# Modulation, first norm and first projections of a hybrid diffusion layer, moved into one block of engine programs

## The reference, cut to what matters

```python
mod = jax.nn.silu(c) @ w_mod[i] + b_mod[i]                 # 1024 -> 6144
mod_c = jax.nn.silu(c_ctx) @ w_mod[i] + b_mod[i]
sh1, sc1, gt1, sh2, sc2, gt2 = jnp.split(mod[:, None, :], 6, axis=-1)
h = rmsnorm(x, norm1_w[i]) * (1 + sc1) + sh1
hc = rmsnorm(ctx, norm1_w[i]) * (1 + csc1) + csh1
y, yc = mixer(h, hc, ...)            # begins with h @ w_in, conv, silu, l2norm, rotary of q, k, v
x = x + gt1 * y
h2 = rmsnorm(x, norm2_w[i]) * (1 + sc2) + sh2
x = x + gt2 * expert_choice_ffn(h2, ...)
# in the mixer, the Fourier branch:
y = jnp.fft.fftn(ug, axes=(1, 3), norm='ortho').real
```

## Time and profile before

| what | value |
|---|---|
| median of three runs | 4763.62 us |
| the profiled execution | 4760.79 us |
| its span (first to last instruction) | 4759.3 us |
| mean granted clock of TensorE over it | 0.936 |
| TensorE, VectorE, ScalarE, GpSimd busy | 86%, 46%, 31%, 9% |
| first projection (L356) starts at | 240.81 us |
| last block of the first tile is copied (L413) at | 273.87 us |

### The profile page before, as it was taken

How to read it: one execution, slowest core, us unless ns; L and a number is a source line. 1 busy time by engine, 2 the same in 40 slices (tenths; PEclk the granted TensorE clock), 3 DMA queues, 4 the chain that set the end, 5 groups by cost and what they waited for, 6 DMA issues and landing times. The chain is left out here.

```text
span 4759.3 us, 62227 instructions
## 1 busy us (share of the span) xinstructions
PE 4105.7 (86%) x22412; PEld 3244.3 (68%) x22412; DVE 2176.2 (46%) x2864; ACT 1498.3 (31%) x2447; POOL 451.1 (9%) x486
## 2 busy tenths in 40 slices
PE   6599997996896299999969999997915999999998
PEld 5244443444674188888857778786815999999997
DVE  0334441005563255555543553534486555555554
ACT  0323331012562022222222332322203444444443
POOL 0000000000011133333300000000000000000000
PEclk9799997998898699999979999998957999999999
DMA  5611112102102322222143434324405666676773
GB/s 209 223 38 58 57 44 78 35 9 67 22 8 56 84 67 78 68 79 79 58 154 120 148 98 158 95 78 166 150 18 191 213 210 214 209 218 201 219 213 102
DMA packets 237491, 546.60 MB, mean 115 GB/s; under 512 B 34154, under 2 KB 103434, under 8 KB 233610
## 3 DMA queue, kind: packets, MB, share of 16 engines
q1 hardware_dynamic: 210890, 446.08, 29.4%
q0 software_dynamic: 26432, 98.06, 6.9%
HBM read 444.25 MB, written 99.81 MB: 114 GB/s over the span
## 5 line engine op out<-in xcount | busy, mean ns | idle before, releaser
L2413 DVE TENSOR_TENSOR sb_we_low<-sb_we,sb_we_high 128x1024 fp32r<-128x1024 f32 x384 | 467.2, 1223 | 142.2 <-ACT sb_we_high L2365 142.0
L2365 ACT ACTIVATE sb_we_high<-sb_we 128x1024 fp32r<-128x1024 f32 x384 | 401.6, 1052 | 292.0 <-PE ey L2338 156.6
L356 PE MATMUL p_ps<-sb_hT,sb_wq 128*128 128x512 f32 (+1 forms) x960 | 380.3, 554 | 32.6 <-DMA sb_wq<-in_w_ch 32.6
L1737 PE MATMUL pg<-sb_hb_high,sb_wm_high 128*128 128x512 f32 x768 | 307.2, 400 | 40.9 <-DVE sb_hb_low L1854 40.9
L1849 DVE TENSOR_TENSOR sb_wm_low<-sb_wm,sb_wm_high 128x1024 fp32r<-128x1024 f32 x128 | 156.3, 1222 | 391.9 <-ACT sb_wm_high L1784 391.9
L356 PEld LDWEIGHTS p_ps<-sb_hT,sb_wq 128*128 128x128 f32 x960 | 184.9, 193 | 219.8 <-issue 180.3
L1738 PE MATMUL pg<-sb_hb_low,sb_wm_high 128*128 128x512 f32 x768 | 303.1, 395 | 0.0
L1739 PE MATMUL pg<-sb_hb_high,sb_wm_low 128*128 128x512 f32 x768 | 302.5, 394 | 0.0
L576 PE MATMUL z_ps<-sb_hT,sb_wz 128*128 128x512 f32 (+1 forms) x672 | 284.6, 587 | 14.8 <-DMA sb_wz<-in_w_ch 14.8
L2320 PE MATMUL eg<-sb_xe_high,sb_we_high 128*128 128x256 f32 x1024 | 289.0, 282 | 2.8 <-DVE sb_xe_low L2408 1.6
L2321 PE MATMUL eg<-sb_xe_low,sb_we_high 128*128 128x256 f32 x1024 | 286.7, 280 | 0.0
(11 more groups left out here) (351 smaller groups left out, 8705.6 us busy)
## 6 DMA issues: line engine op xcount, KB each, us to landing
sb_we<-in_w_ex SPq DMA_DIRECT2D x384, 512.0 KB, 4.4
sb_wm<-in_w_gates SPq DMA_DIRECT2D x96, 512.0 KB, 3.6
sb_wrow<-in_w_mod_row SPq DMA_DIRECT2D x16, 1024.0 KB, 5.1
sb_wm<-in_w_br SPq DMA_DIRECT2D x32, 512.0 KB, 4.5
sb_lq<-q_d SPq DMA_DIRECT2D x36, 256.0 KB, 2.7
sb_lk<-k_d SPq DMA_DIRECT2D x36, 256.0 KB, 2.9
sb_lkt<-kt_d SPq DMA_DIRECT2D x36, 256.0 KB, 3.6
sb_lvt<-vt_d SPq DMA_DIRECT2D x36, 256.0 KB, 4.3
```

The source lines that it names most:

```text
L356: last = nc.tensor.matmul(ps[:, b % BANKS, 0:wd], w[:, kind, k], g.hT[:, k, t0:t0 + wd], start=(k == 0), stop=(k == KD - 1))
L1737: nc.tensor.matmul(bank[:], high, rh[:, k], start=(k == ks[0]), stop=False)
L2365: nc.scalar.activation(wh[:, n % CUT], w[:, n % RAW], ACT.Copy).then_inc(s.wh, 1)
L2413: v.tensor_tensor(wl[:, n % CUT], w[:, n % RAW], wh[:, n % CUT], ALU.subtract).then_inc(s.wl, 1)
```

## The change

`load_tables`, `modulation` and `first_norm` are gone as stages; their work moves into the first window of `delta_inputs`, with no barrier between. In parts:

1. Columns: the two vectors silu(c), silu(c_ctx) become the stationary operand (two columns wide) and w_mod moves past it, 512 columns at a time: 8 x 4 matmuls (`mod_rows`) into four PSUM banks of two partitions. ScalarE and VectorE copy two each to SBUF, and sixteen small transposes turn them to columns (`mod_columns`). w_mod comes in eight DMAs of 1 MB over five slots that lie in tiles not yet used (`sl`, `turned`, `rsb`).
2. Loads: all on SP's queue, in one order: c, five w_mod parts, the first 512 columns of the constants, the small vectors, x of block 0, three more w_mod parts (each waits for a slot), x of block 1, weights of tile 0, x of blocks 2 to 4, weights of tiles 1 and 2, the rest of the constants; the rotary table after the last sum of the norm, since its tile holds the squares.
3. Norm: ScalarE squares a block in two halves, GpSimd adds each half to half its size, TensorE sums four parts instead of eight, ScalarE takes Ln and Exp (for root and reciprocal), VectorE multiplies in two halves; scaling and shifting is split, four parts on ScalarE, four on VectorE. TensorE projects the first tile block by block between the sums.
4. Rows: GpSimd multiplies 64 pieces of w_mod (128x512) by silu(c) per partition and adds them up, seven or eight pieces behind each of the nine weight loads, and stores eight partial rows (`rowp_d`).
5. Fourier loads the partial rows, the bias and norm2; TensorE sums over the partitions with the matrix of ones in eight matmuls, VectorE adds the bias; `rows_d` is stored there.

```diff
--- before.py
+++ after.py
...
-def delta_inputs(nc, g):
+def delta_inputs(nc, g, consts, eps):
...
+flat_sl, flat_tt = sl[:].rearrange("p a t -> p (a t)"), tt[:].rearrange("p n c -> p (n c)")
+wcol = [flat_sl[:, i * 2 * D:(i + 1) * 2 * D] for i in range(3)] + [flat_tt[:, 0:2 * D], rs[:, 0:2 * D]]
+SLOTS = len(wcol)
+sqr = rope[:].rearrange("p a t -> p (a t)").rearrange("p (u k t) -> p u k t", u=2, k=4)
+cols = cv[0:2, 0:2 * D]
 ps = psum(nc, c, "p_ps", (P, BANKS, 512))
...
+prow = [ps[0:2, 0], ps[0:2, 1], ps[0:2, 2], pr[0:2]]
...
+nrs = acc
...
+        def load_x(b):
+            t0, wd = BLOCKS[b]
+            sp.dma_start(g.hT[:, :, t0:t0 + wd], g.xT[:, :, t0:t0 + wd]).then_inc(s_x[b], 16)
+        sp.dma_start(cc[:], g.cc).then_inc(s.cld, 16)
+        for k in range(KD):
+            if k == SLOTS:
+                sp.dma_start(consts[:, 0:C_DIR], g.consts[:, 0:C_DIR]).then_inc(s.cst, 16)
+                sp.dma_start(bcol[:], g.b_mod_col).then_inc(s.small, 16)
+                sp.dma_start(n1[:], g.norm1).then_inc(s.small, 16)
+                load_x(0)
+            if k >= SLOTS:
+                sp.wait_ge(s.used, k - SLOTS + 1)
+            sp.dma_start(wcol[k % SLOTS], g.w_mod_col[:, k]).then_inc(s_wc[k % SLOTS], 16)
+        load_x(1)
+        sp.dma_start(w[:, 0], g.w_ch[0]).then_inc(s_wi[0], 16)
+        for b in range(2, NB):
+            load_x(b)
+        for kind in range(1, 3):
+            sp.dma_start(w[:, kind], g.w_ch[kind * H]).then_inc(s_wi[kind], 16)
         sp.dma_start(cw[:], g.conv_w).then_inc(s.tab, 16)
+        sp.dma_start(consts[:, C_DIR:C_W], g.consts[:, C_DIR:C_W]).then_inc(s.rest, 16)
+        sp.wait_ge(s.nsumh, 2 * NB)
         sp.dma_start(rope[:], g.rope).then_inc(s.tab, 16)
+        for b, (t0, wd) in enumerate(BLOCKS):
+            if b:
+                sp.wait_ge(s.ha, KH * (b + 1))
+                sp.wait_ge(s.hd, KH * (b + 1))
+                sp.dma_start(g.h_d[:, :, t0:t0 + wd], g.hT[:, :, t0:t0 + wd]).then_inc(s.hst, 16)
...
+        def add_squares(b):
+            wd = BLOCKS[b][1]
+            for j in range(2):
+                pool.wait_ge(s.nsq, 2 * b + j + 1)
+                nc.gpsimd.tensor_tensor(sqr[:, j, 0:2, 0:wd], sqr[:, j, 0:2, 0:wd], sqr[:, j, 2:4, 0:wd],
+                                        ALU.add).then_inc(s.nadd, 1)
+        def load_row(i):
+            k, at = i % KD, i // KD * 512
+            pool.dma_start(wrow[:, i % 2], g.w_mod_row[at // (2 * D) * KD + k][:, at % (2 * D):at % (2 * D) + 512]).then_inc(s_wr[i % 2], 16)
+        def row_part(i):
+            k, j = i % KD, i // KD
+            dst = acc[:, j % 2]
+            pool.wait_ge(s_wr[i % 2], 16 * (i // 2 + 1))
+            if k == 0:
+                if j < 2:
+                    pool.wait_ge(s.nmul, 2 * NB)
+                if j >= 2:
+                    pool.wait_ge(s_as[j % 2], 16 * (j // 2))
+                nc.gpsimd.tensor_scalar(dst, wrow[:, i % 2], cs[:, k, 0:1], None, ALU.mult).then_inc(s.part, 1)
+            else:
+                nc.gpsimd.tensor_scalar(wrow[:, i % 2], wrow[:, i % 2], cs[:, k, 0:1], None, ALU.mult).then_inc(s.scaled, 1)
+                pool.wait_ge(s.part, i)
+                pool.wait_ge(s.scaled, i - j)
+                nc.gpsimd.tensor_tensor(dst, wrow[:, i % 2], dst, ALU.add).then_inc(s.part, 1)
+            pool.wait_ge(s.part, i + 1)
+            if i + 2 < ROWP:
+                load_row(i + 2)
+            if k == KD - 1:
+                pool.dma_start(g.rowp_d[:, j * 512:(j + 1) * 512], dst).then_inc(s_as[j % 2], 16)
+        ROWP = 8 * KD
+        for b in range(NB):
+            add_squares(b)
+        tiles = [(h, kind) for h in range(H - 1) for kind in range(3)]
+        load_row(0)
+        load_row(1)
+        for n, (h, kind) in enumerate(tiles):
+            pool.wait_ge(s.proj, NB * (3 * h + kind + 1))
+            pool.dma_start(w[:, kind], g.w_ch[kind * H + h + 1]).then_inc(s_w[kind], 16)
+            for i in range(ROWP * n // len(tiles), ROWP * (n + 1) // len(tiles)):
+                row_part(i)
...
+            if isinstance(t, int) and t == 0:
+                pe.wait_ge(s.ha, KH * (b + 1))
+                pe.wait_ge(s.hd, KH * (b + 1))
...
+        def mod_rows():
+            pe.wait_ge(s.sc, 1)
+            for k in range(KD):
+                pe.wait_ge(s_wc[k % SLOTS], 16 * (k // SLOTS + 1))
+                for j in range(4):
+                    last = nc.tensor.matmul(prow[j], cs[:, k], wcol[k % SLOTS][:, j * 512:(j + 1) * 512],
+                                            start=(k == 0), stop=(k == KD - 1))
+                last.then_inc(s.used, 1)
+        def mod_columns():
+            pe.wait_ge(s.rowe, 4)
+            for m in range(2 * KD):
+                last = nc.tensor.transpose(pcol[:, m], cols[:, m * P:(m + 1) * P], g.ident[0:2, 0:2])
+            last.then_inc(s.colt, 1)
+        def norm_sums(b):
+            wd = BLOCKS[b][1]
+            wait(pe, s.nln, b - 1)
+            for j in range(2):
+                pe.wait_ge(s.nadd, 2 * b + j + 1)
+                for i in range(2):
+                    last = nc.tensor.matmul(pn[:, b % 2, 0:wd], g.ones, sqr[:, j, i, 0:wd],
+                                            start=(j == 0 and i == 0), stop=(j == 1 and i == 1))
+                last.then_inc(s.nsumh, 1)
         def window(new, one, two):
+            if new and not one:
+                mod_rows()
+                pe.wait_ge(s.cst, 16)
+                norm_sums(0)
+                mod_columns()
+                norm_sums(1)
+                norm_sums(2)
             for b in range(NB):
+                if new and not one and 0 < b < 3:
+                    norm_sums(b + 2)
                 if new:
                     project(*new, b)
                 if two and two[1] < 2 and b > 0:
...
+        act.wait_ge(s.cld, 16)
+        nc.scalar.activation(cs[:], cc[:], ACT.Silu).then_inc(s.sc, 1)
+        def squares(b):
+            t0, wd = BLOCKS[b]
+            act.wait_ge(s_x[b], 16)
+            for j in range(2):
+                wait(act, s.nsumh, 2 * (b - 1) + j + 1)
+                nc.scalar.activation(sqr[:, j, :, 0:wd], g.hT[:, j * KH:(j + 1) * KH, t0:t0 + wd], ACT.Square).then_inc(s.nsq, 1)
+        def inverse_root(b):
+            t0, wd = BLOCKS[b]
+            act.wait_ge(s.nsumh, 2 * b + 2)
+            wait(act, s.nmul, 2 * (b - 1))
+            nc.scalar.activation(nrs[:, b % 2, 0:wd], pn[:, b % 2, 0:wd], ACT.Ln, bias=g.eps[:, 0:1], scale=1.0 / D).then_inc(s.nln, 1)
+            act.wait_ge(s.nln, b + 1)
+            nc.scalar.activation(nrs[:, b % 2, 0:wd], nrs[:, b % 2, 0:wd], ACT.Exp, scale=-0.5).then_inc(s.nrs, 1)
+        def modulate(b):
+            t0, wd = BLOCKS[b]
+            which = 1 if b == 0 else 0
+            act.wait_ge(s.mod, 3)
+            act.wait_ge(s.nmul, 2 * b + 1)
+            for k in range(KH):
+                nc.scalar.activation(g.hT[:, k, t0:t0 + wd], g.hT[:, k, t0:t0 + wd], ACT.Identity,
+                                     bias=g.mod1[:, 0, k, which:which + 1],
+                                     scale=g.mod1[:, 1, k, which:which + 1]).then_inc(s.ha, 1)
...
         def window(new, one, two):
+            if new and not one:
+                squares(0)
+                for j in range(2):
+                    act.wait_ge(s.used, KD)
+                    nc.scalar.activation(cols[:, j * 512:(j + 1) * 512], prow[j], ACT.Copy).then_inc(s.rowe, 1)
+                act.wait_ge(s.eps, 1)
+                for b in range(1, NB + 2):
+                    if b < NB:
+                        squares(b)
+                    if b == NB + 1:
+                        act.wait_ge(s.zero, 1)
+                        copy_raw(*new, (0,))
+                    if b > 1:
+                        modulate(b - 2)
+                    if b <= NB:
+                        inverse_root(b - 1)
+                copy_raw(*new, range(1, NB))
+                return
             if new:
...
+        for j in range(2, 4):
+            dve.wait_ge(s.used, KD)
+            nc.vector.tensor_copy(cols[:, j * 512:(j + 1) * 512], prow[j]).then_inc(s.rowe, 1)
...
+        for b, (t0, wd) in enumerate(BLOCKS):
+            which = 1 if b == 0 else 0
+            dve.wait_ge(s.nrs, b + 1)
+            for j in range(2):
+                part = g.hT[:, j * KH:(j + 1) * KH, t0:t0 + wd]
+                nc.vector.tensor_tensor(part, part, nrs[:, b % 2, None, 0:wd].broadcast_to([P, KH, wd]), ALU.mult).then_inc(s.nmul, 1)
+            dve.wait_ge(s.nmul, 2 * b + 2)
+            for k in range(KH, KD):
+                nc.vector.tensor_scalar(g.hT[:, k, t0:t0 + wd], g.hT[:, k, t0:t0 + wd], g.mod1[:, 1, k, which:which + 1],
+                                        g.mod1[:, 0, k, which:which + 1], ALU.mult, ALU.add).then_inc(s.hd, 1)
         dve.wait_ge(s.tab, 32)
...
+        sp.dma_start(parts, g.rowp_d).then_inc(s.rp, 16)
```

(37 more changed lines are left out.)

190 lines of the change are left out of this document (23 added, 167 removed).

## The result

The changed kernel took **4623.31 us** (median of 4 runs, 4617.05 to 4625.03) against 4763.41 (4 runs), 0.9708 of the kernel before, interval [0.9696, 0.972]. The gain is 140 us, not 171; 4623 is just outside the range of 4581 to 4620. The profiled execution took 4625.03, its span is 4623.5. The front did what was forecast and a little more. Most of what is missing went 3.4 milliseconds later, in a stage that the change doesn't touch.

What follows compares the result with a forecast made beforehand. TensorE bounds the windows; a chain of engines working one at a time bounds the start. 4760.8 - 171.4 (block 4's earlier copy) + 3 (rotations) = 4592.4, said as 4592; range 4581 to 4620, own range 4583 to 4600 (62%).

Steps and rivals of the forecast that it cites:

- E: End of the column matmuls (`mod_rows`): 36.8 us, bounds 34 if fast from the start and 61.3 if slow throughout.
- the slow start: Column matmuls: TensorE runs at the slow clock for the first 5.8 us, adding 2.9 us to E.
- slow-columns rival: Columns: narrow stationary operand does not bring the clock up, E = 61.3, +24.5 us, 4617 in all; chance 15%.
- shared-landing rival: Columns: w_mod parts in flight share the engines and land together, 12 us later, 4605 in all; chance 7%.
- the walk: Norm and first projections, timed from E: ScalarE slowest at 10.6 us a block, block 4 copied at E + 65.7 = 102.5.
- slow start of 2.9 behind that wait: Projection of block 3: after 5.6 us idle awaiting block 0's copy, TensorE starts slow, +2.9 us.
- under 4: Sign to look for in the profile: GpSimd's row pieces take under 4 us each.
- The +3 for rotations: Windows: GpSimd's additions delay VectorE's last rotation before the transposes, once per head, +3 us within 0 to 11.
- contention rival: Windows: GpSimd and VectorE hold each other up at full price in rotations, +11 not +3, 4600 or 4611; chance 10%.
- at 0: Fourier stage: summing the partial rows takes 8 to 16 us in a gap of 86.67 us, so no cost.
- the rival said 25 to 40: Norm not run before columns, or first tile not before norm's end: 25 to 40 us of gain lost; chance 4%.
- My own mark: Wrong if the stretch from block 4's copy to the next stage's first projection is over 10 us longer.

Runs made afterwards that it cites:

- 155 early: Changed kernel with 155 more instructions in TensorE's program, in the Fourier stage's wait, restoring the code places of later loops: 4587.22 us.
- p_nopieces: Changed kernel with TensorE's code at the places of before and only the first of every eight GpSimd row pieces kept: 4586.76 us.

## Why the prediction was wrong, step by step

- **Columns**: E forecast at 36.8, measured 36.2. The first part landed at 6.66 and not 6.4, and the slow start cost 2.0 us (eight records in 5.40 for 3.43) and not 2.9. The slow-columns rival and the shared-landing rival are out. Sixteen transposes took 1.15, not 4.4: two columns each, and I had priced them by 128.
- **Norm**: ScalarE's period forecast 10.6, measured 10.36, and its copy of block 0 ended at 85.28, where the walk has it (36.2 + 49). The 3 us by which block 4's copy came sooner (99.4 for 102.5) are the slow start of 2.9 behind that wait, which did not come, and 0.6 of the columns. What the walk had wrong was TensorE's part: 5.6 idle us ahead of block 3, measured 0.56 here and 1.8 in the profiles in which block 1 kept its pace. TensorE had waited before, for GpSimd's sums (up to 3.0 us at a time), and projected block 2 at 77.7 and not at 72.7. The slow matmuls of block 1 (8.27 for 7.03) came out of this wait and cost the front nothing: with 7.03 there (155 early) the copy came 63.4 us behind the columns, and here 63.2. VectorE's and GpSimd's holding each other up (6.65 for 4.48, 7.01 for 4.64) was missing in the walk, and ScalarE just hid it.
- **Rows on GpSimd**: forecast 2.5 us a piece and "under 4". An undisturbed piece is 3.4 us, since the multiplication, priced at half the addition, takes longer than it:

```profile
123.98 1.57 POOL L253 TENSOR_SCALAR sb_wrow<-sb_wrow,sb_cs 128x512 f32<-128x512 f32 x1
125.70 1.26 POOL L256 TENSOR_TENSOR sb_acc<-sb_wrow,sb_acc 128x512 f32<-128x512 f32 x1
127.26 0.56 POOL L239 DMA_DIRECT2D sb_wrow<-in_w_mod_row  x1 [0.30 <-POOL sb_acc L256]
```

  On the average over the windows, VectorE's disturbance in it, a piece is 4.4 us busy (283.4 us for 64). It still fits because the room was large (up to 6.8 us a piece), not because the price was right. The +3 for rotations measured none: from copy to next stage 488.8 us for 490.6 before, and TensorE's waits for the rotations are 6.5 us in 3 in both. The contention rival is out by `p_nopieces`.
- **Fourier**: at 0, within 2.2 us.
- **Parts of the gain**: rows 55.9 us (64 matmuls of 0.858 us are 54.9), overlap 34.0 (the rival said 25 to 40).
- **The step that failed** is the sum itself: 4760.8 - 171.4 + 3. It lets a gain in the first 100 us stand to the end, and treats every stage behind as untouched: what the change does to them is a term put at nothing without a reason, and no rival has it. Of the difference of 31 us, +33.6 arose in `experts` and +3.5 in `merge`, by where TensorE's code fell in its blocks; the delta rule and Fourier add 3.6, and the front gave back 3.1 + 4.8 (the sooner copy; rotations at +3 that were -1.8), for the profiled executions 4592.4 + 33.6 + 3.5 + 3.6 - 7.9 = 4625.2, where 4625.03 was measured. With the places restored the same kernel takes 4587, 5 below the forecast and inside its own range (the slow start of 2.9 and the +3 were priced and did not come). My own mark, over 10 us in the stretch up to the next stage, looked at the wrong end.

## What to carry to other kernels

A change that alters the number of instructions of an engine moves all later loops of that engine in their code blocks. Where a wait for "issue" shows at a loop's jump back, look for a packet of the instruction queue inside it, and move the loop's start with instructions put where the engine idles, so that it stands behind a block's end and not ahead of it. Here 16 did that and were worth 31 us; standing 40 ahead of the end was not enough (7 us lost). Compare stage by stage, not only at the place of the change: the table above finds such a loss in one reading. Before an edit takes work off an engine at the price of waits, see whether that engine keeps its clock.

## What the runs showed of the hardware

- A loop of TensorE that begins about 8 instructions ahead of a block's end cost 2.0 to 4.6 us of stall at each of six jumps back, mostly with 13 to 28 matmul records at a clock of 0.50 behind it: 24 to 34 us in the stage. With 40 instructions ahead of the end the stage lost 7 us, with 109 (the kernel before) it had 1.0 us of such waits. Inside every stall lies one 16 KB instruction packet, and TensorE goes on 1.2 to 1.6 us after it has landed. The taken branch itself took 3.6 to 4.6 us with or without stalls, nearly hidden behind matmuls that run on.
- The Trainium skill ("Runtime: NRT & Kernel Launch", "Instruction fetch mechanics") says that a taken branch to code outside the present pages forces a fetch and a stall, and that crossing a block is mostly hidden. The trace agrees with the first: one packet lies between each branch and the first matmul behind it, and the branch takes 3.9 us in place of 0.08. The second holds here for the other blocks of the loop, of which no wait for "issue" speaks, and not for the one that ends within some 40 instructions behind a jump.
- TensorE's clock stayed at 1.00 with 63.69 of 64.10 us busy and was 0.95 with 52.38 of 63.10 (0.97 in two other profiles): here the lighter load ran slower.
- VectorE and GpSimd lengthened each other, both sides: 4.48 to 6.65 us and 1.92 to 5.88 for VectorE in the norm, 10.59 to 13.29 in a convolution, 4.64 to 7.01 for GpSimd's additions. They took turns. In block 1 of the norm a multiplication of VectorE ended at 57.31, an addition of GpSimd begun at 56.86 at 59.52, VectorE's second multiplication at 61.67, GpSimd's second addition at 63.87: each of the last three ends 2.1 to 2.2 us after the one before it on the other engine, about the 2.2 to 2.3 that it takes undisturbed. The kernel's time did not show it.
